# A hybrid decoder step: six slots of sampled keys move from the attention units to the tiles of v

## The chip, the cores and the metric

The kernel runs on one core of a Trainium2 chip. The core has TensorE (PE: matrix products; PEld: its weight loads), VectorE (DVE), ScalarE (ACT), GpSimd (POOL) and the sync engine SP, which here only issues transfers. Sixteen DMA engines serve the queues of SP (q1), ScalarE (q10) and GpSimd (q0). The metric is the device time of one execution in microseconds, the median of some runs.

## The reference

One inference step of a decoder layer for two groups of requests with shared weights: a prompt of 1024 tokens, and 8 sampled sequences of 4 new tokens each with 2048 past tokens, whose keys and values lie in pages of 128 tokens. What matters here is the attention of the sampled sequences and of the prompt:

```python
def fox_attend(q, k, v, c_q, c_k, q_pos, k_pos):
    s = jnp.einsum('bqhd,bkhd->bhqk', q, k) * (DH_A ** -0.5)
    s = s + jnp.transpose(c_q, (0, 2, 1))[..., :, None] - jnp.transpose(c_k, (0, 2, 1))[..., None, :]
    s = jnp.where(k_pos[None, :] <= q_pos[:, None], s, -jnp.inf)
    p = jax.nn.softmax(s, axis=-1)
    return jnp.einsum('bhqk,bkhd->bqhd', p, v)

def fox_sample(q, k, v, logf, k_past, v_past, logf_past):
    k_all = jnp.concatenate([k_past, k], axis=1)
    v_all = jnp.concatenate([v_past, v], axis=1)
    c_all = jnp.cumsum(jnp.concatenate([logf_past, logf], axis=1), axis=1)
    ...
    return fox_attend(q, k_all, v_all, c_all[:, past_len:], c_all, q_pos, k_pos)
```

There are 8 heads of 64. The past is 8 x 16 pages of keys and as many of values, 256 pages of 128 x 512 float32 (0.26 MB each, 67 MB). After this come an RWKV-7 mixer, a gated mix, and a mixture of experts.

## The kernel before

The function `stage_fox` is the first of the kernel's stages. It has one program for each engine, written out by hand and joined by semaphores; each engine runs its own in order. In time:

1. **Projections** (to 140 us): eight blocks of q and k, TensorE with the normed input `xnT`. The input is also stored to memory (`xn_rows`), since its place is used for pages later and the next stage needs it again.
2. **Tiles of v** (140 to 209 us): nine tiles t of 128 tokens. `values_of(t)` (L503) makes v, `turn_keys(t)` (L515) turns k for the output, VectorE keeps it (`keep_keys`), SP stores k and v.
3. **Attention units** (209 to 427 us): 32 units u, four pairs of heads p by eight blocks of the prompt, in the order 7, 0, 6, 1, 5, 2, 4, 3; block t has (t+1) x 128 keys. Of a unit TensorE does `turn_probs(u, 0)` (L567, L574), `scores(u + 1)` (L554, L557), `turn_probs(u, 1)`, then the unit's sampled slots, then `mix(u)` (L592: turned probabilities with v). VectorE adds the bias (`bias`, L870) and scales the probabilities (`normalise`, L876, L877); ScalarE does the exponential (`weigh`) and copies the turned probabilities (`keep_low`, L745).

The **sampled slots** are put into the units. The sequences come in two groups g of four. A group is eight slots of keys (`keys(g, n)`, L642, eight pages each), one slot "first" which turns probabilities (`turn_sample`, L613), and eight slots of values (`values(g, n)`, L613 and L665, eight pages each): 34 slots, 32 with pages. `slots_of(u)` gives each unit one and units 9 and 17 two. After the last keys of a group VectorE takes own scores and the maximum (L910 to L929) and ScalarE the exponential of all sampled scores. Each value slot of group 0 also has a sum over the forget gates of group 1 on VectorE (`sum_gates`, L835), for which `load_gates(sp, 1)` (L324) must have landed. It writes over the gates of group 0 and so waits for `d_biased`, and stands in SP's order after the page with number 88.

**Pages.** Even pages are loaded by SP (L360), odd ones by GpSimd's indirect transfers (L408). They lie in a ring of 26 places: 10 of their own (`pages`) and 16 over `xnT` (tile `rows`), which is free when the last tile of v is made. The first 10 are loaded early, the next 16 after the tiles of v, and each further one when the slot 26 pages before it is used (`pages_used`). When the last slots are used SP loads the normed input back in four parts (`xn_back`, L400). The first of the next stage's weights come behind it in the same queue (L1017), and TensorE starts with them (L1047).

## Time and profile before

| | us |
|---|---|
| median of 3 runs | 1973.31 |
| lowest and highest | 1968.9, 1974.41 |
| profiled execution | 1972.29 |
| its span | 1970.6 |
| TensorE busy | 1773.7 (90%) |
| VectorE busy | 694.5 (35%) |
| ScalarE busy | 396.1 (20%) |
| GpSimd busy | 221.2 (11%) |

The profiled execution is 1.0 us under the median; between its span and its own time lie 1.7 us. The busy time of TensorE is modelled for matmuls that overlap, so it is the gaps that tell of waits. The granted clock is a share: 1.00 is 2.4 GHz and 0.50 is 1.2 GHz. A wait is put down to the semaphore that came last; "issue" means that the profile shows no releaser, which is so for pages, since several transfers share a semaphore.

### The profile page before, as it was taken

Reading aid. Unit: us, or ns where it says so; the run is one execution under the profiler, and the core shown is the slowest. Engines: PE = TensorE matmul, PEld = TensorE weight load, DVE = VectorE, ACT = ScalarE, POOL = GpSimd, SP = SyncE. Lnnn points to the kernel's source line nnn. Section 1 sums busy time; section 2 is a strip of 40 time slices with the busy share of each in tenths; the row PEclk is TensorE's granted clock in tenths of the full one; section 3 lists DMA queues with packets and bytes.
Section 4 is the critical chain, followed back from the end, with each engine's and each line's share of the span. In section 5 each row is a group of like instructions: output and inputs, shape, how many; then the busy total and the mean of one; then the engine's idle time right before and its main releaser. Section 6 shows DMA issues by size and latency. Waiting matters only on the chain. (4 is left out here: it accounts for less than half of the span.)

```text
span 1970.6 us, 35644 instructions
## 1 busy us (share of the span) xinstructions
PE 1773.7 (90%) x15302; PEld 1058.4 (54%) x15302; DVE 694.5 (35%) x1541; ACT 396.1 (20%) x821; POOL 221.2 (11%) x218
## 2 busy tenths in 40 slices
PE   6999889879999699999999999799999839999980
PEld 4654455548788566666766666464555413333320
DVE  3212456532555723233333323224322421111116
ACT  3001344422232211111111111112010101111112
POOL 2000466520000000000000000000000131111100
PEclk9999999999999899999999999889899859999995
DMA  5601899871100011011111010442430049999946
GB/s 197 221 1 62 282 333 363 324 266 33 32 33 28 7 54 42 27 45 35 38 45 42 27 42 17 189 155 66 151 151 33 33 168 350 397 396 406 391 166 274
DMA packets 83902, 291.66 MB, mean 148 GB/s; under 512 B 16521, under 2 KB 25609, under 8 KB 73217
## 3 DMA queue, kind: packets, MB, share of 16 engines
q1 hardware_dynamic: 63312, 228.59, 30.9%
q0 software_dynamic: 19280, 56.53, 7.9%
q10 hardware_dynamic: 1152, 4.26, 0.6%
q8 instruction: 122, 2.00, 0.4%
q14 instruction: 36, 0.29, 0.0%
HBM read 253.69 MB, written 43.50 MB: 151 GB/s over the span
## 5 line engine op out<-in xcount | busy, mean ns | idle before, releaser
L1284 PE MATMUL gate_p<-rows,gate_w 128*128 128x352 f32 x768 | 280.7, 486 | 1.4 <-DMA gate_w<-in_w_in 1.4
L1047 PE MATMUL rw_pp<-rows,rw_w 128*128 128x264 f32 x896 | 204.3, 389 | 8.4 <-DMA rw_w<-in_w_in 8.4
L1047 PEld LDWEIGHTS rw_pp<-rows,rw_w 128*128 128x128 f32 x896 | 170.6, 191 | 40.4 <-DMA rw_w<-in_w_in 8.6
L1284 PEld LDWEIGHTS gate_p<-rows,gate_w 128*128 128x128 f32 x768 | 129.4, 189 | 55.4 <-issue 2.4
L1961 PE MATMUL x_p<-late 128*128 128x512 f32 (+1 forms) x288 | 128.7, 601 | 2.6 <-PEq L182 2.6
L2230 PE MATMUL moe_gu<-wgu,rows 128*32 128x512 f32 (+1 forms) x640 | 125.0, 617 | 2.8 <-DMA wgu<-in_we_gu 1.5
L2230 PE MATMUL moe_gu<-late,rows 128*32 128x512 f32 (+1 forms) x640 | 122.6, 599 | 0.0
L1506 DVE TENSOR_TENSOR tl<-tl,scan_zb 128x256 f32<-128x256 f32 x64 | 26.9, 421 | 192.9 <-PE scan_zb L1298 192.9
L1961 PEld LDWEIGHTS x_p<-late 128*128 128x128 f32 (+1 forms) x288 | 51.6, 184 | 67.4 <-issue 67.4
L1438 ACT COPY ys<-scan_yp 128x256 f32<-128x256 f32 x80 | 29.8, 372 | 222.9 <-PE scan_yp L1298 222.9
L2230 PEld LDWEIGHTS moe_gu<-wgu,rows 128*32 128x32 f32 (+1 forms) x640 | 30.2, 117 | 71.8 <-issue 60.6
L1298 PEld LDWEIGHTS scan_yp<-tl,ltm 64*64 64x64 f32 x1280 | 43.6, 134 | 41.4 <-DVE tt L1507 33.5
L870 DVE CUSTOM_DVE_ANT_0 fox_work<-fox_a,fox_work 128x1024 f32<-128x1024 f32 (+7 forms) x64 | 47.0, 754 | 52.3 <-PE fox_a L557 38.2
L1654 POOL MEMSET empty<- 128x1056 int32 x1 | 1.0, 978 | 565.2 <-POOLq L1205 565.2
L1298 PE MATMUL scan_yp<-tl,ltm 64*64 64x64 f32 x1280 | 53.9, 223 | 7.9 <-DVE tt L1507 5.0
L1663 PE MATMUL mix_b<-rows,mix_wa 128*128 128x512 f32 x128 | 60.6, 629 | 0.0
L2442 DVE TENSOR_SCALAR obT<-moe_yp,moe_ent 128x512 f32<-128x512 f32 x24 | 18.0, 750 | 118.6 <-PE moe_yp L2242 118.6
L2242 PE MATMUL moe_yp<-late,moe_aT 128*32 128x512 f32 (+1 forms) x320 | 58.1, 594 | 0.5 <-DVE moe_aT L2437 0.5
L408 POOL DMA_INDIRECT rows<-in_cache_kT,page_index x34 | 36.2, 1064 | 197.7 <-PE fox_a L503 179.1
L2242 PE MATMUL moe_yp<-wd,moe_aT 128*32 128x512 f32 (+1 forms) x320 | 58.3, 596 | 0.0
L1663 PE MATMUL mix_b<-obT,mix_wb 128*128 128x512 f32 x128 | 55.4, 593 | 0.0
L2030 POOL DMA_INDIRECT expert_table<-ent,slot x18 | 17.8, 988 | 318.8 <-DVEq L2145 313.9
(404 smaller groups left out, 2884.4 us busy)
## 6 DMA issues: line engine op xcount, KB each, us to landing
wgu<-in_we_gu SPq DMA_DIRECT2D x16, 2048.0 KB, 14.2
late<-in_we_gu SPq DMA_DIRECT2D x16, 2048.0 KB, 10.7
wd<-in_we_down SPq DMA_DIRECT2D x16, 1024.0 KB, 9.8
late<-in_we_down SPq DMA_DIRECT2D x16, 1024.0 KB, 12.5
rows<-in_cache_v SPq DMA_DIRECT2D x44, 256.0 KB
gate_rows<-u_rw SPq DMA_DIRECT2D x60, 176.0 KB, 1.9
rows<-in_cache_kT SPq DMA_DIRECT2D x34, 256.0 KB
mix_gate<-gate_rows SPq DMA_DIRECT2D x16, 528.0 KB, 4.1
```

The source lines that it names most:

```text
L408: return pool.indirect_dma_start(out=out, out_offset=None, in_=source, in_offset=bass.IndirectOffsetOnAxis(ap=index[:, column:column + 1], ...
L870: dve.tensor_tensor_reduce(prob[:, u % 2, s, 0:n], score[s][:, 0:n], ckb[:, p % 2, s, 0:n], -0.125, 3.0e38, ALU.add, ALU.min, stat[:, u % ...
L1047: mm = pe.matmul(pp[u % 2][:, c, 0:QN], w[:, n % 2, k, :], e.xnT[:, k, at:at + QN], start=(i == 0), stop=(i == KD - 1))
L1284: mm = pe.matmul(out[:, 0:GATE_N], gw[:, j % 2, k, :], e.xnT[:, k, at], start=(k == 0), stop=(k == KD - 1))
L1298: mm = pe.matmul(out(p, hs), lhsT(p, hs), rhs(p, hs), start=start, stop=stop)
L1438: act.copy(ys[:], ypv).then_inc(q["kept_y"], 1)
L1506: dve.tensor_tensor(tl[:], tl[:], zp[:, :, 0, :], ALU.subtract)
L1663: mm = pe.matmul(banks[n % NBK][:], weights[:, k], src[:, k, at:at + HN], start=(k == 0), stop=(k == HP - 1))
L1961: mm = pe.matmul(xp[t % 2][0:n, c], e.mixedT[:, k, t * P:t * P + n], wo[:, k, c * 512:(c + 1) * 512], start=(k == 0), stop=(k == KD - 1))
L2230: mm = pe.matmul(gu[d][at:at + n, :], hT[:, d, k, at:at + n], wgu[u][:, k, :], start=(k == 0), stop=(k == KD - 1))
L2242: mm = pe.matmul(yp[at:at + n, c], aT[:, d, k, at:at + n], wd[u][:, k, c * 512:(c + 1) * 512], start=(k == 0), stop=(k == 1))
L2442: dve.tensor_scalar(y[:, t % NW, 512:D], yp[:, 1], weight(t), None, ALU.mult).then_inc(y_dve, 1)
```

## The change

Six of the eight key slots of group 0 (AHEAD = 6) are taken out of the attention units and done by a new function `keys_ahead(n)` between the tiles of v. Their scores go into a free bank of `fox_a` (`ahead`), and VectorE reads them there (`score_ahead(n)`). The pages of these 48 have places of their own: slots 0, 2 and 4 in eight of the kept places, slots 1, 3 and 5 over the weights of q and k (`over_w`, in tile `rows`), which are spent after the last projection. A slot waits until the slot two before it is used. The ring of 26 begins after them with page 48 (LATER); its first 10 pages wait for the fifth slot's use. SP's loads stand in its loop over the tiles. `slots_of(u)` becomes one slot a unit from the seventh on, so that units 0 to 27 have one and units 28 to 31 none; no unit has two. The part `xn_back` 0 waits for 31 used slots and the others for 32. The number of matmuls, pages and vector operations is the same.

```diff
+AHEAD = 6
+LATER = AHEAD * SLOT
...
+        def pair(i):
+
+            if i < LATER:
+                i = i % (2 * SLOT)
+                return kept_pages[:, i:i + 2] if i < SLOT else over_w[:, i - SLOT:i - SLOT + 2]
+            i = (i - LATER) % RING
+            return kept_pages[:, i:i + 2] if i < PAGES_KEPT else over_xn[:, i - PAGES_KEPT:i - PAGES_KEPT + 2]
...
+        def wait_place(eng, i):
+
+            if i < LATER:
+                if i // SLOT == 1:
+                    eng.wait_ge(made, 2 * HP)
+                elif i // SLOT >= 2:
+                    eng.wait_ge(pages_used, i // SLOT - 1)
+            elif i < LATER + RING:
+                eng.wait_ge(pages_used, AHEAD - 1)
+            else:
+                eng.wait_ge(pages_used, (i - RING) // SLOT + 1)
...
         def slots_of(u):
 
-            double = (TT + 1, 2 * TT + 1)
-            first = u + sum(x < u for x in double)
-            return range(first, first + 1 + (u in double))
+            return range(AHEAD + u, min(AHEAD + u + 1, len(SLOTS)))
...
-            for i in range(0, PAGES_KEPT, 2):
+            for i in range(0, SLOT, 2):
                 load_page(i)
             sp.wait_ge(lf_stored, 16)
             load_gates(sp, 0)
+            for i in range(SLOT, 2 * SLOT, 2):
+                load_page(i)
             for t in range(NTT):
                 n, at = size(t), slice(t * P, t * P + size(t))
+                if 2 <= t < AHEAD:
+                    for i in range(t * SLOT, (t + 1) * SLOT, 2):
+                        load_page(i)
+                if t == AHEAD + 1:
+                    for i in range(LATER, LATER + PAGES_KEPT, 2):
+                        load_page(i)
                 sp.wait_ge(k_kept, t + 1)
...
-            for i in range(PAGES_KEPT, RING, 2):
+            for i in range(LATER + PAGES_KEPT, LATER + RING, 2):
                 load_page(i)
...
-            for i in range(RING, len(SLOTS) // 17 * 16 * SLOT, 2):
+            for i in range(LATER + RING, len(SLOTS) // 17 * 16 * SLOT, 2):
                 if i == RING + CHUNKS * SLOT:
                     sp.wait_ge(d_biased, 1)
                     load_gates(sp, 1)
                 load_page(i)
...
-            for b, used in ((3, 30), (0, 32), (1, 32), (2, 32)):
+            for b, used in ((0, 31), (1, 32), (2, 32), (3, 32)):
...
+            def keys_ahead(n):
+                if n == 0:
+                    pe.wait_ge(qs_ready, 2 * HP)
+                    pe.wait_ge(z_ready, 1)
+                else:
+                    pe.wait_ge(d_scored, n)
+                pe.wait_ge(even_loaded[n], 8 * SLOT)
+                pe.wait_ge(odd_loaded[n], 8 * SLOT)
+                for p in range(HP):
+                    for b in range(BG):
+                        mm = pe.matmul(ahead[32 * b:32 * b + 32, :].rearrange("q (j n) -> q j n", j=2), qs[:, b, p, :],
+                                       pair(n * SLOT + 2 * b)[:, :, p * P:(p + 1) * P], start=(p == 0), stop=(p == HP - 1))
+                mm.then_inc(pages_used, 1)
...
             turn_keys(2)
+            keys_ahead(0)
             values_of(3)
...
             mm.then_inc(logf_turned, 1)
+            keys_ahead(1)
             for t in range(4, NTT):
                 values_of(t)
                 turn_keys(t - 1)
+                if t - 2 < AHEAD:
+                    keys_ahead(t - 2)
             turn_keys(NTT - 1)
...
             for t in range(3, NTT):
                 keep_keys(t)
+                if t - 1 < AHEAD:
+                    score_ahead(t - 1)
```

The line numbers in the orders below are those of each kernel's own text. TensorE's order from the tile of v with number 1 on, before (L503 is `values_of`, L515 `turn_keys`, L531 and L534 turn the forget gates):

```order
62 L503 MATMUL fox_a<-fox_work,rows 128x512 [waits v_kept]
63 L503 MATMUL fox_a<-fox_work,rows 128x512 x7
64 L515 MATMUL fox_b<-const,qk 128x128 x8
65 L503 MATMUL fox_b<-fox_work,rows 128x512 [waits v_kept]
66 L503 MATMUL fox_b<-fox_work,rows 128x512 x7
67 L531 MATMUL fox_a<-const,fox_work 128x8 [waits logf_ready]
68 L531 MATMUL fox_a<-const,fox_work 128x8 x7
69 L531 MATMUL fox_a<-const,fox_work 32x8
70 L534 MATMUL fox_a<-fox_work,const 32x4 x8
71 L503 MATMUL fox_a<-fox_work,rows 128x512 [waits v_kept]
```

The same place in the changed kernel (L519 is `values_of`, L531 `turn_keys`, L544 `keys_ahead`):

```order
64 L531 MATMUL fox_b<-const,qk 128x128 x8
65 L544 MATMUL fox_a<-pages,qs 32x256 [waits even_pages_loaded0,odd_pages_loaded0,z_ready,qs_ready]
66 L544 MATMUL fox_a<-pages,qs 32x256 x15
67 L519 MATMUL fox_b<-fox_work,rows 128x512 [waits v_kept]
68 L519 MATMUL fox_b<-fox_work,rows 128x512 x7
69 L562 MATMUL fox_a<-const,fox_work 128x8 [waits logf_ready]
70 L562 MATMUL fox_a<-const,fox_work 128x8 x7
71 L562 MATMUL fox_a<-const,fox_work 32x8
72 L565 MATMUL fox_a<-fox_work,const 32x4 x8
73 L544 MATMUL fox_a<-rows,qs 32x256 [waits odd_pages_loaded1,even_pages_loaded1,dec_scored]
74 L544 MATMUL fox_a<-rows,qs 32x256 x15
75 L519 MATMUL fox_a<-fox_work,rows 128x512 [waits v_kept]
```

A group of 16 key products (32 records in the trace) now stands between the turned keys and the next tile of v.

VectorE's order where it first uses the gates of group 1, before, in unit 9 (L870 bias, L892 keeps turned sampled probabilities, L835 sums gates, L876 and L877 scale):

```order
163 L870 ISA fox_work<-fox_a,fox_work 128x896 [waits fox_scored,fox_turned_hi,fox_turned_lo]
164 L870 ISA fox_work 128x1
165 L870 ISA fox_work<-fox_a,fox_work 128x896 [waits fox_scored]
166 L870 ISA fox_work 128x1
167 L892 COPY dec_probT<-fox_b 128x256 [waits side_made]
168 L835 SCALAR_TENSOR_TENSOR gates<-ones,gates 128x256 [waits gates_loaded]
169 L892 COPY dec_probT<-fox_b 128x256 [waits side_made]
170 L835 SCALAR_TENSOR_TENSOR gates<-ones,gates 128x256 [waits gates_summed]
171 L876 RECIPROCAL fox_work<-fox_work 128x1 [waits fox_exped]
172 L877 TENSOR_SCALAR fox_work<-fox_work 128x896 [waits dve_steps]
```

In the changed kernel, in unit 3 (L912 bias, L934 keeps, L866 sums, L918 and L919 scale):

```order
109 L912 ISA fox_work<-fox_a,fox_work 128x768 [waits fox_scored,fox_turned_hi,fox_turned_lo]
110 L912 ISA fox_work 128x1
111 L912 ISA fox_work<-fox_a,fox_work 128x768 [waits fox_scored]
112 L912 ISA fox_work 128x1
113 L934 COPY dec_probT<-fox_b 128x256 [waits side_made]
114 L866 SCALAR_TENSOR_TENSOR gates<-ones,gates 128x256 [waits gates_loaded]
115 L918 RECIPROCAL fox_work<-fox_work 128x1 [waits fox_exped]
116 L919 TENSOR_SCALAR fox_work<-fox_work 128x768 [waits dve_steps]
```

The first use of the gates stands six units earlier, with one sum in the unit in place of two. SP's order around the load of these gates is, in the changed kernel as before, with the pages in front of it of values and not of keys:

```order
213 L375 DMA rows<-in_cache_v 128x512
214 L371 TENSOR_LOAD table
215 L371 ISA x2
216 L375 ISA [waits pages_used]
217 L375 DMA rows<-in_cache_v 128x512
218 L342 DMA gates<-lf_rows 32x1x2048 [waits dec_biased]
219 L342 DMA gates<-lf_rows 32x1x2048 x3
220 L371 TENSOR_LOAD table
```

Before, the same row numbers hold the same four transfers, after the same page 88. What stands between the end of the tiles of v and these gates is less than before: 16 of SP's pages in place of 40.

TensorE's order at the end of the stage, before (unit 31; L567 turns probabilities, L615 to L671 a slot of values, L592 `mix`, L623 the sampled output):

```order
611 L567 MATMUL fox_b<-const,fox_work 128x128 [waits fox_kept_lo,fox_weighed]
612 L567 MATMUL fox_b<-const,fox_work 128x128 x3
613 L615 MATMUL fox_b<-const,dec_prob 32x128 [waits fox_out,side_kept]
614 L665 MATMUL fox_b<-rows,dec_probT 32x512 [waits odd_pages_loaded7,even_pages_loaded7,side_kept]
615 L665 MATMUL fox_b<-rows,dec_probT 32x512 x7
616 L671 MATMUL fox_b<-v_tok,dec_probT 32x512 [waits side_kept]
617 L671 MATMUL fox_b<-v_tok,dec_probT 32x512 x3
618 L592 MATMUL fox_b<-fox_work,v_tok 64x128 [waits fox_kept_lo,side_kept,fox_out]
619 L592 MATMUL fox_b<-fox_work,v_tok 64x128 x7
```

In the changed kernel (L602 turns, L627 `mix`, L658 the sampled output):

```order
575 L602 MATMUL fox_b<-const,fox_work 128x128 [waits fox_kept_lo,fox_weighed]
576 L602 MATMUL fox_b<-const,fox_work 128x128 x3
577 L602 MATMUL fox_b<-const,fox_work 128x128 [waits fox_kept_lo,fox_weighed]
578 L602 MATMUL fox_b<-const,fox_work 128x128 x3
579 L627 MATMUL fox_b<-fox_work,v_tok 64x128 [waits fox_kept_lo,side_kept,fox_out]
580 L627 MATMUL fox_b<-fox_work,v_tok 64x128 x7
581 L658 MATMUL fox_b<-const,fox_work 128x128 [waits dec_out]
```

The slot of values between the second turning and `mix` is gone, in this unit and in the three before it.

## Rows read from the trace of the kernel before

**Rows 1.** Busy time by stretches: from:to, length, engines (instructions), clock, DMA, GB/s

```profile
175.00:209.60 34.60, 34.60 (x99) 14.89 (x97) 3.01 (x5) 3.16 (x6) 0.08 (x1) 1.00 0.27 92
209.60:240.00 30.40, 23.12 (x240) 14.25 (x238) 17.38 (x48) 13.24 (x31) 21.32 (x20) 0.94 0.94 320
240.00:270.00 30.00, 27.90 (x347) 17.19 (x348) 16.72 (x55) 14.58 (x32) 19.31 (x18) 0.94 1.03 372
```

**Rows 2.** TensorE's waits, 209.5 to 427.5 us: who for whom, sum us, times, longest

```profile
PE fox_b L567 <- DVE fox_work L877: 13.4, 14, 3.9
PE fox_b L592 <- DVE dec_probT L892: 3.4, 2, 2.3
PE fox_b L642 <- issue: 2.9, 2, 2.4
PE fox_b L642 <- DVE dec_stat L919: 1.2, 1, 1.2
```

**Rows 3.** Timeline, TensorE, a tile of v: start, us, group, [idle before <-releaser]

```profile
164.44 7.03 PE L503 MATMUL fox_b<-fox_work,rows 128*128 128x512 f32 x16
```

**Rows 4.** Timeline, TensorE, a slot of keys and what follows it

```profile
231.83 1.93 PE L642 MATMUL fox_b<-rows,qs 128*32 128x256 f32 x32
233.70 1.75 PE L592 MATMUL fox_b<-fox_work,v_tok 128*64 128x128 f32 x28
```

**Rows 5.** Timeline, TensorE, the start of a slot of values and what follows the slot

```profile
287.12 0.38 PE L613 MATMUL fox_b<-const,dec_prob 128*128 128x128 f32 x2
...
289.29 1.75 PE L592 MATMUL fox_b<-fox_work,v_tok 128*64 128x128 f32 x28
```

**Rows 6.** Unit 3's slot of keys, unit 4's start (TensorE), and the stretch between

```profile
240.11 0.38 PE L642 MATMUL fox_b<-rows,qs 128*32 128x256 f32 x1 [2.37 <-issue]
...
244.65 0.66 PE L567 MATMUL fox_b<-const,fox_work 128*128 128x128 f32 x4 [0.39 <-DVE fox_work L877]
...
240.00:244.00 4.00, 3.89 (x40) 2.30 (x40) 0.53 (x4) 0.59 (x2) 0.00 (x0) 0.58 1.04 389
```

**Rows 7.** Timeline, SP's queue of issues, pages 26 to 48

```profile
229.63 4.71 SPq L360 DMA_DIRECT2D pages<-in_cache_kT  x5
235.10 6.89 SPq L360 DMA_DIRECT2D rows<-in_cache_kT  x7
```

**Rows 8.** Timeline, SP's issues of the gates, group 0 and group 1

```profile
87.50 2.96 SPq L324 DMA_DIRECT2D gates<-lf_rows  x4
...
270.75 2.84 SPq L324 DMA_DIRECT2D gates<-lf_rows  x4
```

**Rows 9.** Stretches after group 0's gates, amid group 1's gates, and before 240 us

```profile
95.50:98.00 2.50, 2.50 (x10) 1.65 (x9) 0.01 (x1) 0.00 (x0) 0.00 (x0) 1.00 0.01 3
...
278.00:280.00 2.00, 1.94 (x17) 0.42 (x16) 2.00 (x5) 1.17 (x3) 0.00 (x0) 1.00 0.52 217
...
235.00:240.00 5.00, 2.75 (x24) 1.37 (x18) 2.15 (x5) 2.37 (x6) 3.75 (x4) 1.00 1.04 397
```

**Rows 10.** Timeline, VectorE, the first sum of group 1's gates and a scaling

```profile
282.18 0.69 DVE L835 TENSOR_TENSOR_SCAN gates<-ones,gates 128x256 f32<-128x256 f32 x1 [1.86 <-DMA gates<-lf_rows]
...
283.94 0.69 DVE L877 TENSOR_SCALAR fox_work<-fox_work 128x896 f32<-128x896 f32 x1
```

**Rows 11.** Timeline, TensorE, unit 31's second turning

```profile
421.34 0.63 PE L567 MATMUL fox_b<-const,fox_work 128*128 128x128 f32 x4 [0.82 <-ACT fox_work L745]
```

**Rows 12.** Timeline, the next stage's start: TensorE, SP's input and weights

```profile
435.79 1.69 PE L1047 MATMUL rw_pp<-rows,rw_w 128*128 128x264 f32 x3 [8.36 <-DMA rw_w<-in_w_in]
...
423.99 1.28 SPq L400 DMA_DIRECT2D rows<-xn_rows  x3
429.40 0.34 SPq L1017 DMA_DIRECT2D rw_w<-in_w_in  x1
```

**Rows 13.** Transfers issued 30 to 56 us (KB, us to landing); a later stretch

```profile
rows<-in_w_in SPq DMA_DIRECT2D x2, 512.0 KB, 3.1
...
434.00:439.00 5.00, 3.21 (x8) 2.56 (x9) 0.00 (x0) 0.00 (x0) 0.00 (x0) 0.54 0.64 219
```

More of the change, by code:

```diff
@@ L292, in stage_fox @@
         pt_lo, pt_hi, op, side = fb[:, 0], fb[:, 1], fb[:, 2, 0:P], fb[:, 2, 2 * P:4 * P]
-        dec = fb[:, 3]
+        dec, ahead = fb[:, 3], fa[:, 2, 0:2 * P]
         size = lambda t: min(P, NT - t * P)
@@ L432, in _ @@
             pool.wait_ge(index_set, 1)
-            for i in range(1, PAGES_KEPT, 2):
+            for i in range(1, LATER + PAGES_KEPT, 2):
                 load_page(i)
@@ L436, in _ @@
             pool.wait_ge(spilled, 16)
-            for i in range(PAGES_KEPT + 1, RING, 2):
+            for i in range(LATER + PAGES_KEPT + 1, NB * NPG * 2, 2):
                 load_page(i)
-            for x in range(len(SLOTS)):
-                kind, g, n = SLOTS[x]
-                if kind != "first":
-                    first = RING + page_slot(g, kind, n) * SLOT
-                    for i in range(first + 1, min(first + SLOT, NB * NPG * 2), 2):
-                        load_page(i)
         @block.tensor
@@ L836, in sum_gates, with score_ahead @@
                                        ALU.mult, ALU.subtract).then_inc(gates_summed, 1)
+            def score_ahead(n):
+                at = slice(2 * n * P, 2 * n * P + 2 * P)
+                dve.wait_ge(gates_summed, n + 1)
+                dve.wait_ge(pages_used, n + 1)
+                dve.tensor_tensor_reduce(prob_d[:, at], ahead, gates[:, at], -0.125, 3.0e38, ALU.add, ALU.min,
+                                         stat_d[:, n:n + 1]).then_inc(d_scored, 1)
             for c in range(CHUNKS):
@@ L851, in _ @@
             keep_keys(2)
+            score_ahead(0)
             dve.wait_ge(logf_turned, 1)
```

21 lines of the change are left out of this document (7 added, 14 removed).

## The prediction

> **What bounds the kernel now.** I read the busy table by stretches first [rows 1]. While the tiles of v are made (175 to 209.6 us) TensorE is busy without a gap and the DMA engines are nearly idle (share 0.27). In the attention part (209.6 to 427.5 us) it is the reverse: the DMA share is 0.94 and 1.03 in its first 60 us, and TensorE has holes (23.12 of 30.4 us busy). The reader should then ask the waits of TensorE how much of those holes the pages cause [rows 2]. All its waits there come to 24.4 us (nine lines; the four largest stand in the group); 13.4 us are for the probabilities that VectorE scales, L877, and 3.4 us for VectorE's copy of turned probabilities. Those that can be pages are the two before L642, 2.9 us: TensorE idles from 237.7 to 240.1 and then runs at half clock (granted 0.58 from 240 to 244) [rows 6]. So the attention part is bound by TensorE and by the softmax chain between two of its groups; the DMA engines are full, but only about 4 us of waiting show it.
>
> **Part 1, keys in the tiles of v.** A slot of keys is 32 records in column quarters that run beside each other. From its start to the start of the next group it takes 231.83 to 233.70, 1.87 us [rows 4]. A tile's 16 products take 7.03 us and stand back to back with what follows [rows 3]; TensorE has no idle time from 175 to 209.6 [rows 1], so nothing there hides a slot: 6 x 1.87 = 11.2 us are added before the attention part. The waits in front of the six slots cost nothing: the pages of a slot have two places, a tile with its slot and its turned keys takes some 9.4 us, and eight pages are 2.1 MB, 5.6 us at the 372 GB/s of the full DMA engines [rows 1]; SP issues four pages at 1.09 us and Pool four at about 1.3 us. They have a tile of margin. VectorE adds 0.42 us a slot, beside 7 us of TensorE. SP passes its four pages before it waits for the turned keys, so no store of k is late.
>
> **Part 2, the first four units.** Unit 0 and unit 1 keep a slot of keys, as before. Unit 1's is now the last of the group, whose VectorE work (own scores, maximum) is six operations in place of one and, by the trace at unit 7, 1.0 us longer: unit 2 starts 1.0 us late. Unit 2 has only a turning. Unit 3 has the first slot of values, 2.17 us (287.12 to 289.29) [rows 5], and after it VectorE does the first sum over the forget gates of the second group, for which those gates must have landed. They go over the old ones after the last keys of group 0, and SP issues them after the page before them in its order. That order is untouched, and this is the point on which I spend most care. I give times here on the clock of before; the changed kernel is 11.2 us later at the same point. SP loads eight pages from 229.63 on, 1.09 us apart, without waiting (five and then three of the next seven) [rows 7]; in the changed kernel the same eight stand there, and the gates follow at 237.7. Before, they went at 270.75 and VectorE took them at 282.18, 11.4 us later, with pages in front and 1.86 us of waiting [rows 8, 10]. Without anything in front they went at 87.50 and the traffic ends at 95.5: 8 us [rows 8, 9]. They move at half of the DMA share (0.52 with 217 GB/s) [rows 9], each writing 32 partitions of 128. So they land between 245.5 and 249.1. SP's eight pages, issued over the 8 us before, are still in its queue (share 1.04 until 240) [rows 9], so I take 248.8, near the loaded end. VectorE is ready at 240.8: unit 3's slot stands where the keys of 237.7 stood, 0.9 us later, then biases for unit 4 of 2 x 0.95 us. Wait: 8.0 us (bounds 4.7 and 8.3). Behind it in VectorE's order stand the scaled probabilities of unit 4, for which TensorE waits: the sum of gates 0.7, a reciprocal 0.16 and the scaling 0.7 (durations as in [rows 10]) put unit 4 at 250.4. Before, with the wait for pages, it started at 244.65 [rows 6]. The wait for pages (2.4 us) goes, since unit 2 takes none, and a longer one for the gates comes: **+5.7 us** for this stretch, though a slot of keys less stands in it.
>
> **Part 3, unit 4 to the end.** Before this took 244.65 to 427.43 (435.79 less 8.36), 182.8 us [rows 6, 12]. What leaves: four slots of keys (7.5 us), one of values (2.17 us), one turning (0.3 us), 10.0 us. The gaps there change too: 24.4 us less 7.8 before unit 4 (3.9, 1.1, 2.4 and 0.4) leaves 16.6 now. The two units with a double slot go: in one TensorE waited 1.18 us for its own second slot's place [rows 2] and 0.7 us more for scaling, in the other 1.5 us round the gates: -3.4. VectorE's copy of turned probabilities had TensorE wait twice, 1.1 and 2.3 us [rows 2]: the first is now in part 2, and the second stands before a tile of 768 keys, not 1024 (2.3 us becomes 1.7): -1.7; unit 8's start loses the 0.7 us of the own-score work. In the last four units nothing stands between the turned probabilities and their use. There TensorE waits for ScalarE's copy, as unit 31 does already: 0.82 us [rows 11]; I count 0.7, 0.8, 0.75 and 0.85 in the four, 0.8 and 0.15 for scaling, and 1.2 us before unit 28, behind the scaling of the sampled output that stood at the very end: +5.3 with what was there taken off (0.84). Gaps after: 16.1. So the stretch becomes 182.8 - 10.0 - 0.5 = 172.3: **-10.5 us**. The slots that leave the last four units are 9.6 us of TensorE (four of values and the sample's own) and give 4.3; that is what lost cover costs.
>
> **Part 4, the next stage.** Its first weights are issued at 429.40 and land behind three parts of the normed input, issued at 423.99 because the last slot of values was the last unit's: TensorE starts at 435.79 after 8.36 us, 6.4 us after the issue [rows 12]. After the change the parts go four units earlier and are done (3.2 MB, 8 us). A weight of this size with a free queue took 3.1 us [rows 13], so TensorE starts near 432.6: -3.2. The clock is at half from 434 to 439 in most of the time (0.54) [rows 13]; I expect a shorter such stretch that begins while TensorE already works, and give 0.2 back: **-3.0 us**.
>
> **A rule of the Trainium skill.** What the rows show: in the attention part 372 GB/s at a DMA share of 1.03, and some 4 us of waiting for pages [rows 1, 2, 6]. The Trainium skill, Perfetto Trace Analysis, section Identifying the Most-Contended Engine, has one judge by the occupancy, for DMA by the use of HBM, and work on that one first. By that the part is bound by transfers, and the 12.6 MB that go into the idle tiles would give back up to 12.6/0.372 = 34 us. The waits speak against it; it is a rival below.
>
> **Sum.** 11.2 + 5.7 - 10.5 - 3.0 = +3.4 us on the profiled execution's 1972.3 us (span 1970.6): 1975.7. The runs shown have a median of 1973.3 (1968.9 to 1974.4), 1.0 above it; the forecast for the median is 1976.5. A measurement of this kernel tells about 0.3%, 5.9 us, from no change.
>
> **Rivals.**
> - *As summed* (0.50): 1971 to 1980, the wait for gates between 4.7 and 8.3 us, the clock stretches in the same number.
> - *Faster, the gates are in time* (0.14): if SP's queue is drained by 240 the gates take the 8 us of the free case, and if TensorE or VectorE is later than I think at unit 3 by some us, nothing is left of the wait. Point: landing before 243 on the clock of before. Then unit 4 starts at 243 in place of 250.4, 7 us less: 1969, with 1964 if the clock stretch after it goes too (half of 3.4 us). Against it: eight pages just ahead in the same queue.
> - *Faster, bound by transfers* (0.04): the attention part shortens by the bytes taken out, 34 us less 11.2 us of tiles: about 1950. For it the full DMA share; against it only 2.9 us of possible page waits [rows 2].
> - *Slower, units without a slot stay as long* (0.22): the chain of bias, exponential, scaling and copy, not TensorE, sets the length of a unit, so that taking slots out shortens nothing. Place: the last four units; they give 0 in place of 4.3 us, and with more idle time a clock stretch at half (3.4 us, costs 1.7) falls into them: 1982. It decides if the chain from the end of the scores to scaled probabilities passes about 3.5 us there; for 1024 keys it is 3.9 us on idle engines at the start [rows 2], for 384 to 640 I work with 1.7 to 2.6.
> - *The change doesn't do what it says* (0.10): pages for a slot between tiles come late, because SP stands in one order with the stores of k and v. TensorE then waits in the tiles; price 2 us a slot for four slots, 1984. Against it the margin of a tile.
>
> **How the numbers follow.** The likeliest is 1976.5. To keep at most 2 in 10 outside, the range goes down into the case with the gates in time and up to the long last units: 1965 to 1984; the first case's own is 1971 to 1981. Faster by over 0.3% (below 1967.4): most of the transfer case and half of the gates case, and a little of the first, 0.14. Slower by over 0.3% (above 1979.2): two thirds of the fourth and the fifth case and a sixth of the first, 0.30. Within: 0.56.
>
> **What would show it.** In the changed kernel's trace: (1) tiles of v 9.4 us apart, the first scores 11 us later, near 221; (2) a wait of VectorE for the gates of 5 to 8 us at about 252 to 260 and a gap of TensorE of 6 to 9 us before unit 4, where before there were 1.86 us; no wait before a slot of keys near 248; (3) no gap of over 1.2 us at units 9 and 17; (4) gaps of 0.7 to 0.85 us before the use of v in units 28 to 31; (5) the next stage's first product 5.2 us after the last of this one, in place of 8.4. If (2) is missing the forecast is 7 us too high; if the waits before the keys in the tiles are over 0.5 us each, part 1 is wrong; if the last four units take over 23 us together (24.7 before, 20.4 by my sum), part 3 is.

## The result and the profile after

The changed kernel takes 1977.56 us (median of 20 runs, 1971.48 to 1983.27), the kernel before 1970.38 us (20 runs, 1968.09 to 1974.41): a ratio of 1.0036, with a 95% interval of 1.0028 to 1.0043. It is 7.2 us slower. (The ratios in this document are estimates over all the runs of a set; they can differ by up to 0.001 from the quotient of the two medians.) The forecast was 1976.5 us in a range of 1965 to 1984. The number is met to 1.1 us, the difference is not: +3.4 us were forecast and +7.2 came. The number is near only because the median of before, over 20 runs, is 2.9 us below that of the three runs that the forecast started from. Which of the recorded outcomes came is not clear cut. The time lies below the 1979.2 us that the prediction wrote down as the bound of "slower" (0.30); the ratio lies just above 0.3%, with an interval that holds 0.3%. That the change makes the kernel slower is clear; that it does so by more than 0.3% is not. The profiled execution has a span of 1977.1 us, 6.5 us more than that of before.

The first three places to look at are the tiles of v, the start of unit 4 and the end of the stage. In the changed kernel the products of a tile are L519, a slot of keys between tiles L544, a unit's scores L589 to L592, the turnings L602 and L609, the mix with v L627, a slot of values L696. Timeline of TensorE over the last two tiles of v (start us, us, engine, line, operation, tiles, form, count, idle time before it and what ended it):

```profile
201.80 1.93 PE L544 MATMUL fox_a<-pages,qs 128*32 128x256 f32 x32
203.67 7.13 PE L519 MATMUL fox_b<-fox_work,rows 128*128 128x512 f32 x16
210.64 0.60 PE L531 MATMUL fox_b<-const,qk 128*128 128x128 f32 x4
211.17 1.93 PE L544 MATMUL fox_a<-rows,qs 128*32 128x256 f32 x32
212.92 7.03 PE L519 MATMUL fox_a<-fox_work,rows 128*32 128x512 f32 x16
...
220.90 1.99 PE L589 MATMUL fox_a<-qk 64*128 64x512 f32 x8
```

From slot to slot it is 9.37 us, no row carries an idle time, and the first scores start at 220.90. Before, they started at 209.68:

```profile
209.68 1.99 PE L554 MATMUL fox_a<-qk 64*128 64x512 f32 x8
```

Now the rows round unit 4, the answers to [rows 6], [rows 8] and [rows 10]. SP's issue of the gates (L342) and of the pages behind them:

```profile
248.36 2.84 SPq L342 DMA_DIRECT2D gates<-lf_rows  x4
252.84 19.17 SPq L375 DMA_DIRECT2D rows<-in_cache_v  x5
```

VectorE, from its last work for unit 4's biases on:

```profile
252.22 0.42 DVE L934 COPY dec_probT<-fox_b 128x256 f32<-128x256 f32 x1
262.67 0.69 DVE L866 TENSOR_TENSOR_SCAN gates<-ones,gates 128x256 f32<-128x256 f32 x1 [10.03 <-DMA gates<-lf_rows]
...
263.45 0.62 DVE L919 TENSOR_SCALAR fox_work<-fox_work 128x768 f32<-128x768 f32 x1
```

TensorE, from the end of unit 3 to the start of unit 4:

```profile
252.74 0.66 PE L627 MATMUL fox_b<-fox_work,v_tok 128*64 128x128 f32 x8
264.12 1.11 PE L602 MATMUL fox_b<-const,fox_work 128*128 128x128 f32 x4 [10.73 <-DVE fox_work L919]
```

VectorE is through with everything at 252.64 and then stands for 10.03 us until the gates are there; TensorE, which needs the scaled probabilities behind that sum in VectorE's order, stands for 10.73 us. The stretches tell the rest (from:to, length, engines with instructions, granted clock, DMA share, GB/s):

```profile
220.90:252.00 31.10, 24.38 (x255) 15.44 (x258) 17.48 (x51) 14.25 (x31) 16.47 (x16) 0.89 0.95 323
252.00:264.00 12.00, 1.29 (x16) 0.45 (x8) 1.93 (x7) 1.67 (x5) 4.02 (x4) 0.68 0.89 266
264.00:270.00 6.00, 5.88 (x24) 3.56 (x28) 2.86 (x10) 1.95 (x5) 0.00 (x0) 0.50 0.09 33
```

During the wait the DMA engines carry 266 GB/s; then the pages have run as far ahead as their places allow, and almost nothing moves (share 0.09, 33 GB/s). The granted clock has fallen to half while TensorE stood and stays there until 270 us, so that a four-block turning takes 1.11 us in place of 0.66. TensorE at the end of the stage:

```profile
432.45 0.63 PE L602 MATMUL fox_b<-const,fox_work 128*128 128x128 f32 x4 [0.82 <-ACT fox_work L776]
433.85 1.10 PE L627 MATMUL fox_b<-fox_work,v_tok 128*64 128x128 f32 x16 [0.77 <-ACT fox_work L776]
...
436.02 0.41 PE L658 MATMUL fox_b<-const,fox_work 128*128 128x128 f32 x2 [0.71 <-DVE rows L945]
442.28 1.25 PE L1089 MATMUL rw_pp<-rows,rw_w 128*128 128x264 f32 x2 [5.84 <-DMA rw_w<-in_w_in]
```

The next stage begins 5.84 us after this one, where it was 8.36 [rows 12]. In one line, changed against before: +11.22 us to the first scores, +8.25 from there to unit 4 (264.12 less 220.90, against 244.65 less 209.68), -10.46 from unit 4 to the end (436.44 against 427.43), -2.52 to the next stage; the sum is +6.49, the difference of the spans.

### The profile page after: what moved, and what is told of

It is laid out like the page before. It is cut to its first block and busy times, and to the rows that moved or that the text cites. A ratio compares the mean times of both kernels' runs of the same rounds, so it can differ in the third digit from the quotient of the medians.

```text
span 1977.1 us, 35645 instructions
## 1 busy us (share of the span) xinstructions
PE 1774.3 (90%) x15302; PEld 1058.5 (54%) x15302; DVE 695.5 (35%) x1541; ACT 395.4 (20%) x821; POOL 219.9 (11%) x218
## 5 line engine op out<-in xcount | busy, mean ns | idle before, releaser
L912 DVE CUSTOM_DVE_ANT_0 fox_work<-fox_a,fox_work 128x1024 f32<-128x1024 f32 (+7 forms) x64 | 47.1, 754 | 53.9 <-PE fox_a L592 40.5
L602 PE MATMUL fox_b<-const,fox_work 128*128 128x128 f32 x208 | 37.5, 297 | 25.2 <-DVE fox_work L919 23.7
## 6 DMA issues: line engine op xcount, KB each, us to landing
late<-in_we_gu SPq DMA_DIRECT2D x16, 2048.0 KB, 11.2
```

The source lines that it names most:

```text
L602: mm = pe.transpose(pt_lo[:, k * P:(k + 1) * P], prob[:, u % 2, s, k * P:(k + 1) * P], ident)
L912: dve.tensor_tensor_reduce(prob[:, u % 2, s, 0:n], score[s][:, 0:n], ckb[:, p % 2, s, 0:n], -0.125, 3.0e38, ALU.add, ALU.min, stat[:, u % ...
```

## Experiments: is it the wait for the gates?

**Theory A** is that the whole loss is the late landing of the second group's gates, with the clock that falls in the wait. **Rival B**: the pages are late next, and the wait only hides theirs. **Rival C**: the loss is the slots in the tiles and the bare last units. The kernel before ran beside these four with a median of 1970.94 us.

**No gates loaded.**

```diff
-                if i == RING + CHUNKS * SLOT:
-                    sp.wait_ge(d_biased, 1)
-                    load_gates(sp, 1)
...
-                    dve.wait_ge(gates_loaded, 16 * BG * (g + 1))
+                    dve.wait_ge(gates_loaded, 16 * BG)
```

> The changed kernel without the load of the second group's forget gates (left out: that load, so the sampled rows of the second group are scored with the first group's sums; every other instruction stays, the eight sums too). Theory A, the gates' late landing is the whole loss: TensorE's gap before unit 4 (10.73 us in the changed kernel) falls below 1 us and the stretch at half clock behind it (about 3 us of loss) goes with it: 1977.6 - 10 - 3 = 1964.6, range 1963 to 1967, faster than the kernel before by 3 to 7 us. Rival B, the pages are late next: the gap moves to unit 4's or unit 5's slot of values, with 'issue' or a page transfer as its releaser, and comes to over 4 us; 1970 to 1976. Rival C, the loss is the slots in the tiles and the bare last four units: the time stays above 1974.

Measured: 1964.33 us, ratio 0.9968 (0.9956 to 0.9981). VectorE's first sum over the gates (line numbers are three lower in this kernel):

```profile
252.58 0.68 DVE L863 TENSOR_TENSOR_SCAN gates<-ones,gates 128x256 f32<-128x256 f32 x1
```

TensorE, the start of unit 4:

```profile
254.03 0.66 PE L599 MATMUL fox_b<-const,fox_work 128*128 128x128 f32 x4 [0.60 <-DVE fox_work L916]
```

The wait is gone and no other takes its place, though one slot of values now starts 10 us earlier: rival B falls. From unit 4's first turning to ScalarE's copy of its output it is 6.18 us here and 8.86 us in the changed kernel, so the clock at half took 2.7 us there. Rival C falls too: with the same slots in the same places the kernel is 6.6 us faster than the one before. (Without the load the second group's scores are wrong; the run shows times only.) The load itself is left out, so this bounds theory A but does not isolate the wait from the transfer. The next run does.

**The sums two slots later.** All transfers stay; only VectorE asks for them later.

```diff
                 keep_sample(g, n + 1)
-                if g + 1 < NB // BG:
-                    sum_gates(g + 1, n)
+                if g + 1 < NB // BG and n >= 2:
+                    sum_gates(g + 1, n - 2)
...
+                if g and n < 2:
+                    sum_gates(g, CHUNKS - 2 + n)
                 dve.wait_ge(gates_summed, g * CHUNKS + n + 1)
```

> The changed kernel with VectorE's eight sums over the second group's gates two slots later (the first sum behind unit 5's scores in place of unit 3's, the last two beside the first keys of the second group); SP's order and every transfer stay as they are. Theory A: the gates land at 262.7 as before, but unit 4 no longer waits for them; VectorE meets the first sum near 268 and does not wait. The time is that of the run without the load within 1.5 us: 1964 to 1968. Rival B (what comes next in line is late too): above 1970, with a gap of TensorE for pages. Rival D, the gates' transfer is slow only because all else stands still and the pages run ahead beside it: with the units going on, the gates land later than 263 and the wait comes back at unit 5, 3 us or more: 1968 to 1972.

Measured: 1965.45 us, 0.9971 (0.996 to 0.9982). VectorE's first sum is now behind unit 5's scores and waits for nothing:

```profile
263.52 0.69 DVE L866 TENSOR_TENSOR_SCAN gates<-ones,gates 128x256 f32<-128x256 f32 x1
```

TensorE over the same few us, the start of unit 6's turning and its slot of values:

```profile
264.91 0.66 PE L602 MATMUL fox_b<-const,fox_work 128*128 128x128 f32 x4 [0.35 <-DVE fox_work L919]
...
269.23 1.92 PE L696 MATMUL fox_b<-rows,dec_probT 128*32 128x512 f32 x16 [1.51 <-DVE dec_probT L934]
```

The last packet of the gates ended at 262.6, so the sum came just in time. The one new gap, 1.51 us before unit 6's slot of values, is put down to VectorE's copy, which had ended at 268.9; it is more likely a page, since it is absent where the gates are not loaded. That is all there is of rival B. Rival D of the expectation falls too: the last packet comes 14.1 us after the issue, but VectorE does not wait for it. Theory A holds: the place of VectorE's eight sums, of which only the first ever waited, is worth 12 us against the changed kernel (10 us where both ran in one set, below).

**The gates eight pages earlier in SP's order.**

```diff
-                if i == RING + CHUNKS * SLOT:
+                if i == LATER + RING:
                     sp.wait_ge(d_biased, 1)
                     load_gates(sp, 1)
```

> The changed kernel with the second group's gates moved forward in SP's order by eight pages: they are issued as soon as the last own score of the first group is made (241.4 us) in place of 248.36. If the backlog of SP's own queue is what makes the transfer long (8 us free, 11.4 before, 14.3 in the changed kernel), it now takes 8 to 11.4 us, lands at 249.5 to 253, VectorE (ready at 252.6) does not wait, and the time is 1964 to 1967. If it is the share of the DMA engines with all other queues, it takes 14.3 us again: landing at 256, a wait of 3.4 us, the clock still falls behind it for one stretch: 1968 to 1971. Rival: the eight pages that are now behind the gates are late for unit 4: a gap for pages of 2 us or more there.

Measured: 1972.82 us, 1.0014 (1.0003 to 1.0024), 1.8 us above the range of the second of the two cases that were written down (1968 to 1971). SP's issue of the gates:

```profile
243.10 2.84 SPq L342 DMA_DIRECT2D gates<-lf_rows  x4
```

VectorE's first sum over them:

```profile
256.46 0.69 DVE L866 TENSOR_TENSOR_SCAN gates<-ones,gates 128x256 f32<-128x256 f32 x1 [2.16 <-DMA gates<-lf_rows]
```

And the stretch in which unit 4 begins (columns as above):

```profile
258.00:262.00 4.00, 4.00 (x19) 2.59 (x20) 1.58 (x4) 0.68 (x2) 1.76 (x2) 0.57 1.03 373
```

The issue is 5.3 us earlier, and cannot be earlier still: the last own score of group 0, which reads the old gates, is made at about 243. From issue to use it is 13.4 us, as in the changed kernel (14.3) and not 11.4 as before. The wait shrinks to 2.16 us, and a stretch at half clock still follows. Unit 4 still takes 4.4 us longer from output to output than with the sums later (10.57 and 6.16 us), of the 7.4 us between the two medians; the rest stays open.

**The normed input called back late.**

```diff
-                sp.wait_ge(pages_used, used)
+                sp.wait_ge(mixed, NU)
```

> The changed kernel with the four parts of the normed input called back only after the last unit (as late as the kernel before called the last three of them, or later), in place of from unit 25 on. If the early return is the source of part 4's gain, the next stage's first product comes about 8.4 us or more after the last of this one, in place of 5.84: 1977.6 + 2.5 = 1980 to 1982. If the weight itself is the bound, nothing changes: 1977 to 1978.

Measured: 1983.72 us, 1.0065 (1.0052 to 1.0078), and TensorE at the boundary:

```profile
451.09 4.33 PE L1089 MATMUL rw_pp<-rows,rw_w 128*128 128x264 f32 x9 [12.69 <-DMA rw_w<-in_w_in]
```

The gap is 12.69 us in place of 5.84, and the median is 6.2 us above that of the changed kernel. (The profiled execution took 1990.69 us, 7 us above its kernel's median, so its gap may be longer than usual.) The early return is the source of part 4's gain. The loss is larger than the 2.5 us expected. Two differences from the kernel before go that way, and no run parts them: there one part was back earlier and here none is, and there SP issued the other three 3.4 us before TensorE's end of the stage (423.99 against 427.43), here all four 1.4 us before it (437.00 against 438.40).

## Experiments: the length of the transfer, and the number of slots

The next four ran on another chip, on which the kernel before itself took 2001.79 us (23 runs) and not 1970; only ratios within the set are to be compared.

**The gates through ScalarE's queue.**

```diff
-                if i == RING + CHUNKS * SLOT:
-                    sp.wait_ge(d_biased, 1)
-                    load_gates(sp, 1)
...
                     act.wait_ge(d_biased, g + 1)
+                    if g == 0:
+                        load_gates(act, 1)
```

> The changed kernel with the second group's gates issued by ScalarE, at the point where it begins the exponential of the first group's probabilities (about 242 us), and not by SP: a queue of its own with nothing in front. The sums stay where the change has them. If the transfer is long because of SP's queue in front of it (13.4 us from issue to use in the run with the gates moved forward), it now takes about 8 us as alone, lands near 251 and VectorE does not wait; TensorE's gap before unit 4 below 1 us; 1965 to 1968 (ScalarE's four issues cost up to 2.8 us, part of it seen). If the share of the DMA engines makes it long, it lands at 255 to 257 as in that run, with a wait of 2 to 4 us and 1969 to 1973.

Measured: 2001.16 us, 0.9991 (0.9975 to 1.0008). ScalarE's queue of issues:

```profile
242.54 3.35 ACTq L342 DMA_DIRECT2D gates<-lf_rows  x4
```

TensorE, a turning that stands behind ScalarE's copy:

```profile
248.67 0.63 PE L599 MATMUL fox_b<-const,fox_work 128*128 128x128 f32 x4 [3.48 <-ACT fox_work L773]
```

The last packet of the gates ends at 257.4, 14.9 us after the issue, from a queue in which nothing stood in front. So SP's own backlog is not what makes this transfer long; the DMA engines, shared with the pages of the other queues, are the reason that is left (argued, not shown). On this same chip the three kernels that load the gates through SP's queue took 10.2 to 10.5 us from issue to last packet, each at a later place, so the place counts too. VectorE did not wait for the gates, since it reached them only at 259.55, later than in the changed kernel (252.64): TensorE's wait below and the half clock behind it (0.5 from 250 to 256 us) had made the units before late. Neither of the two cases that were written down came as a whole. The four issues cost ScalarE 3.35 us. TensorE waited 3.48 us for the copy behind them, where the changed kernel has no wait; between issues and copy stands the exponential of the sampled scores (2.03 us), which stands there in the changed kernel too. Whether this placement beats the changed kernel can't be said: that kernel did not run on this chip.

**The kernel before with the sums later.** The same edit as above in the kernel before.

> The kernel before with the sums over the second group's gates two slots later, nothing else. VectorE waited 1.86 us for the gates there, TensorE about 1.5 us round them. Theory A says the wait is a loss only where the slots moved ahead bring the sum 18.5 us nearer to the issue: here at most 1.5 us of gain, 1969 to 1970.5, not to be told from the kernel before. If the later sums help the kernel before as much as the changed one (12 us), theory A is wrong and something else in that edit speeds both up.

Measured: 2004.23 us, 1.0003 (0.999 to 1.0016). The edit is worth nothing that can be measured where the sum stood late enough already. This is the control for theory A: the 10 to 12 us belong to the changed order. It is a weaker one than it could be, since on this chip TensorE waits more for other things, which may hide a little.

**Four slots and two slots, sums later.** AHEAD is 4 or 2, and the order in which the input's parts are called back follows from the places that come free (with four, parts 2 and 3 at 30 used slots and parts 0 and 1 at 32).

```diff
-AHEAD = 6
+AHEAD = 2
...
-            for b, used in ((0, 31), (1, 32), (2, 32), (3, 32)):
+            for b, used in ((0, 30), (1, 31), (2, 31), (3, 32)):
```

> The same with four slots between the tiles: two units, 30 and 31, are bare. Against two slots: +3.74 us in the tiles, -4.1 for two slots of values, +2.6 for cover lost in two bare units (half of the 5.3 us of the prediction's part 3), -2.5 for the return of the input, which two more bare units let begin earlier: 1967 again, range 1965 to 1969. If bare units stay as long as covered ones, 1969 to 1971.

> The changed kernel with the sums over the gates two slots later (as in the second experiment) and two slots of keys between the tiles of v in place of six: every unit then keeps exactly one slot, none two and none is bare. Against the kernel before, two slots (3.74 us) move out of the two double units into the tiles; by part 3 of the prediction the double units also gave back 3.4 us of gaps, and part 4 gives nothing, since the last unit has a slot of values as before. Additive theory: 1970.5 - 3.4 = 1967, range 1965.5 to 1969; the next stage's first product about 8 us after the last one. Rival (double units were worth nothing, all gain is the early return of the input): 1970 to 1971.

Measured: four slots 1988.86 us, 0.9939 (0.9921 to 0.9957); two slots 1988.11 us, 0.9933 (0.9912 to 0.9954). On this chip the gain is larger than six slots had given on the other, which could be the number of slots or the chip. So the series was run once more, on one chip, with the changed kernel among it; there the kernel before took 1971.72 us (29 runs).

> The changed kernel itself, on one chip with the three that follow. If the chip moves pages as the one of the profiles of before and after did (350 GB/s in the attention part): 1.0036 of before. If it is one like that of the last four runs (kernel before at 2001.8 us, 302 to 326 GB/s, gaps of TensorE of 42 us in the attention part in place of 24): the 12.6 MB moved into the tiles now count, about 12.6/0.31 - 12.6/0.35 = 5 us more of waiting taken out, and it stands at 0.998 to 1.002 of before.

> The changed kernel with the sums two slots later, again, to stand beside four and two slots on one chip. On a chip with 350 GB/s 0.9971 of before as the first time (0.996 to 0.998); on one with 310 GB/s 0.990 to 0.993, since transfers bind more there. In both 10 to 13 us below the changed kernel: that is the wait for the gates.

> Four slots in the tiles, sums later, again. By the terms of the prediction (3.74 us of tiles, 2 x 2.05 us of values out, 2.6 us of lost cover in, 2.5 us of the input's early return out against two slots; against six slots the return is the same and two slots fewer are moved) it is at most 1.5 us above or below six slots. On a chip with 350 GB/s 0.997 to 0.999 of before, on one with 310 GB/s 0.994 as the first time. If the transfers bind at 310 GB/s, six slots beat four there by 0.1 to 0.3%, and not at 350.

> Two slots in the tiles, sums later, again: no unit with two slots, none bare. By the prediction's 3.4 us for the two double units 0.998 to 0.999 of before on a chip with 350 GB/s (1.000 if the double units were worth nothing), 0.993 as the first time on one with 310 GB/s.

| kernel | median us | ratio to before (95%) | first scores | last unit's output | next stage |
|---|---|---|---|---|---|
| before | 1971.72 | 1 | 209.68 | 425.99 | 435.79 |
| six slots, as changed | 1976.29 | 1.0031 (1.0019 to 1.0042) | 221.10 | 433.31 | 440.88 |
| six slots, sums later | 1966.08 | 0.997 (0.9958 to 0.9982) | 221.96 | 424.46 | 432.05 |
| four slots, sums later | 1965.22 | 0.9968 (0.9956 to 0.9981) | 217.31 | 421.33 | 429.24 |
| two slots, sums later | 1962.07 | 0.9955 (0.9937 to 0.9972) | 213.25 | 421.10 | 428.40 |

(The three columns at the right are times in us in the profiled executions; that of before is the one of the rows ahead. The profiled execution of six slots with the sums later is the slowest of its twelve, 4.5 us above the median; in the kernels with six slots the first scores alone lie between 220.85 and 222.45 us.) The changed kernel is slower than before here too, by 4.6 us in the medians. From the first scores to the last output it is 216.3 us before, then 207.9, 204.0 and 202.5 us with two, four and six slots ahead. The first two slots take out 8.4 us and cost 3.6 in the tiles; the next two take out 3.8 and cost 4.1; the last two take out 1.5 and cost 4.6 (3.74 by part 1, the rest lies ahead of the tiles). Two slots have the lowest median, 3.2 us below four, but the intervals overlap, and on the other chip the two are 0.8 us apart: that they are the best is likely, not shown. The reason that the rows suggest is that they are the two that sat double in a unit; from there on every unit keeps one slot, and a further one only leaves the end, where TensorE then waits. Two slots gained more than the 0.998 to 0.999 that was written down: the first of its two expectations had the next stage start about 8 us after the last product, and it was 5.9. TensorE's waits from 209.5 to 440 us with two slots (who for whom: us in total, times, the longest):

```profile
PE fox_b L602 <- DVE fox_work L919: 13.7, 14, 3.8
PE rw_pp L1091 <- DMA rw_w<-in_w_in: 5.9, 1, 5.9
PE fox_b L627 <- DVE dec_probT L934: 3.4, 2, 2.3
PE fox_b L673 <- issue: 1.6, 1, 1.6
PE fox_b L627 <- issue: 1.4, 3, 0.5
PE fox_b L602 <- ACT fox_work L776: 0.8, 1, 0.8
PE fox_b L658 <- DVE rows L945: 0.7, 1, 0.7
```

The same with six slots:

```profile
PE fox_b L602 <- DVE fox_work L919: 13.2, 13, 3.8
PE rw_pp L1091 <- DMA rw_w<-in_w_in: 6.1, 1, 6.1
PE fox_b L696 <- issue: 2.3, 1, 2.3
PE fox_b L627 <- DVE dec_probT L934: 2.3, 2, 1.2
PE fox_b L627 <- ACT fox_work L776: 2.2, 3, 0.8
PE fox_b L627 <- issue: 1.8, 4, 0.5
PE fox_b L602 <- ACT fox_work L776: 1.4, 2, 0.8
```

With six the waits of L627 and L602 for ScalarE's copy have come in (2.2 and 0.6 us more), and 2.3 us for pages at the start of the values; with two, the slot of keys waits 1.6 us for pages. The boundary gap is 5.9 us already with two, though the last unit has a slot of values as before: two parts of the input are called back one unit earlier than before.

## Why the prediction came out as it did

**Part 1 (+11.2)** measured +11.22: no wait before any of the six slots, tiles 9.37 us apart (9.4 expected, first scores "near 221", 220.90).

**Part 2 (+5.7)** measured +8.25. This is the term that was mis-sized, and the step is "I take 248.8, near the loaded end", with "Wait: 8.0 us (bounds 4.7 and 8.3)". SP issued the gates at 248.36, which is 237.1 on the clock of before (237.7 predicted), VectorE was ready at 252.64 (252.0 predicted), both within 0.7 us; but from issue to use it was 14.3 us, and I had allowed 11.1 and at most 11.4, the one loaded case in the trace. The upper bound was a single sample. The loaded case was counted from issue to use; by its last packet it was 10.8 us. In the runs here the last packet of the gates ends 10.2 to 16.5 us after the issue: 13.4 in the changed kernel and 11.5 in its second profile, 14.9 through ScalarE's queue, 16.5 with four slots on one chip and 10.5 on the other. The wait was 10.03 us (8.61 in the second profile). What I left out of the price altogether is the clock behind the wait: 2.7 us of unit 4 at half clock (1.8 in the second profile), which lies in part 3's stretch. The mechanism, its place and what is queued behind it were right, and the experiment that moves the sum shows that they are the cause.

Where the 8.2 us come from by which VectorE's wait grew (10.03 less 1.86) can be read off as well. The old gates are free when VectorE has the maximum of the group, before and in the changed kernel:

```profile
268.20 0.16 DVE L929 TENSOR_REDUCE dec_stat<-dec_stat 128x1 f32<-128x9 f32 x1
```

```profile
241.25 0.16 DVE L971 TENSOR_REDUCE dec_stat<-dec_stat 128x1 f32<-128x9 f32 x1
```

From there to the moment when VectorE is ready for the new gates it is 12.0 us before and 11.2 after: the same two units stand between, and no more than 0.7 us was lost there. But SP issues the gates 2.4 us after that moment before and 7.0 us after it in the changed kernel, since its pages in front came later (4.6 us), and issue to use takes 14.3 in place of 11.4 us (2.9 us).

**Part 3 (-10.5)** measured -10.46, and is right by luck: two errors cancel. The 2.7 us of half clock in unit 4, and another 1.1 us at half in unit 20 (7.35 us from output to output, 6.27 without the gates), are in it and were not in my sum. In the run without the gates the same stretch goes from 254.03 to 423.92 us, 169.9 us, which is -12.9 with a stretch at half of some 1.6 us of its own in unit 28. (The second profile of the changed kernel has no such stretch in unit 20 and has one in unit 28: where one falls differs between executions of the same kernel.) So the stretch gave 2.4 us beyond the sum. TensorE's gaps in it went from 17.1 to 16.2 us (0.5 less expected) and its busy time from 165.9 to 154.2 us, 11.6 less where I had 10.0. Most of that excess is the clock: the kernel before had two stretches at half there, the run without the gates one. Before:

```profile
322.60:326.00 3.40, 3.40 (x17) 2.85 (x18) 1.75 (x4) 0.59 (x1) 2.36 (x3) 0.50 1.03 380
377.20:380.60 3.40, 3.40 (x22) 2.52 (x19) 1.67 (x4) 1.02 (x4) 0.00 (x0) 0.50 0.59 223
```

Without the gates:

```profile
403.00:406.40 3.40, 3.40 (x15) 1.99 (x14) 1.16 (x3) 0.59 (x1) 0.00 (x0) 0.50 1.01 427
```

TensorE is busy all through, so each costs half of its 3.4 us. The double units gave about what the sum says: units 8 to 10 and 15 to 18 of before took 22.8 and 32.4 us, with two slots ahead 19.1 and 28.5, 7.7 us together, where my sum had 3.7 us of slots and 3.4 of gaps. The four bare units took 19.6 us by TensorE (24.7 before, 20.4 by my sum). The gaps in them stand as predicted: 0.66 to 0.88 us, and 1.08 before unit 28 (1.2).

**Part 4 (-3.0)** measured -2.52: the gap is 5.84 us (5.2 expected). SP issued the weight at 438.40, 1.96 us after the stage's end as before, and TensorE had it 3.9 us later, where I had taken 3.1 from a free queue.

**The number.** The parts add up to +3.4 us and came to +6.5; 2.55 of the 3.1 us between them are part 2. That the forecast of 1976.5 lies so near 1977.56 is luck: what the sum lacked, the three runs that it started from had too much. My sum and its 1.0 us for the median give 1976.7, and 8 us after 237.7 is 245.7, not 245.5; neither slip matters. The first case came in kind, but outside its bounds: the wait was to be at most 8.3 us, with the clock stretches in the same number.

**The rivals.** "The gates are in time" did not come by itself, but its price is confirmed: I gave 1969 and 1964 with the clock, and the runs that take the wait out gave 1964.33 and 1965.45 us. "Units without a slot stay as long" is wrong in its size and right in its direction: the four shorten by 5 us (24.7 to 19.6), but the four slots cost 7.5 us in the tiles. The half clock that it put into the bare units did come in the second profile, where unit 28 takes 7.44 us and not 5.86. The fifth and sixth slot together lose about 3 us in the profiled executions; in the medians (1965.22 and 1966.08) that cannot be told from nothing. "The change doesn't do what it says" did not show. "Bound by transfers" is wrong where I looked: 4.2 MB moved with two slots gave 8.4 us and the next 8.4 MB 5.4 us, where a constant rate of 0.372 MB per us would give 11 and 23 us. The Trainium skill, Perfetto Trace Analysis, section Identifying the Most-Contended Engine, has one optimize the most contended engine first, and judges DMA by its HBM utilization. Read as in the prediction, that would have had the part follow the bytes. The runs disagree by the numbers just given, and the waits of TensorE that can be pages were 2.9 us before.

**Slower by over 0.3% had 0.30.** With a half clock priced into the first case and a transfer of 11 to 15 us, the sum would have been 1977.5 to 1983 by my estimate (up to 3.9 us more of wait, 1 to 2.7 of clock), and the chance of "slower" about even.

## What to carry to other kernels

When a step is taken out of a chain, look for what had been given its time by that step: here SP reached the issue of the gates 7.0 us after their place was free and not 2.4, the transfer took 2.9 us longer, and the use stood in front of everything else on VectorE's order. Let the consumer of a transfer stand as late in its engine's order as its own reader allows; two slots later cost nothing and gave 10 to 12 us. And of work that is moved into another stage, move first what stands doubled. What was alone in its unit was cover for a wait: here the third to sixth slot took 5.4 us out of the units and cost 8.7 us ahead of them.

## What the runs showed of the hardware

- A load of 1 MB in four transfers, each to 32 partitions, took 10.2 to 16.5 us from the first issue to the last packet beside other traffic (12 loads through SP's queue; 14.9 us in the one through ScalarE's); alone, for the first group, it took 7.7 to 8.8 us in the same profiles (8.3 in the kernel before). In the changed kernel the DMA engines moved 266 GB/s at a share of 0.89 meanwhile.
- A wait of TensorE of 10.7 us was followed by some 6 us of work at half clock, 2.7 us of loss; in the second profile of the same kernel a wait of 9.3 us was followed by 4 us of such work, 1.8 us of loss. With a wait of 2.86 us before unit 4 (the gates eight pages earlier) the clock was at half from about 258 to 261 (0.57 over four us) as well.
- One chip of those used ran the kernel before in 2001.79 us and not in 1971. The kernel with two slots ran on both kinds: its profiles have spans of 1992.3 and 1959.3 us, and most of the difference lies before the next stage's first product (458.93 and 428.40 us). From 280 to 340 us the transfers stood at 314 GB/s with a DMA share of 0.91 on that chip, and at 347 and 0.97 on the usual one. The stretch on the first chip, and on the usual one:

```profile
280.00:340.00 60.00, 49.54 (x471) 26.82 (x473) 34.24 (x95) 23.66 (x59) 36.62 (x35) 1.00 0.91 314
```

```profile
280.00:340.00 60.00, 54.66 (x541) 30.40 (x537) 39.92 (x116) 27.36 (x67) 38.89 (x37) 0.97 0.97 347
```

  There the same edits paid more (two slots 0.9933 and 0.9955, four 0.9939 and 0.9968; the intervals overlap). What limits that chip stays open: its DMA engines were less busy, not more.
